# A streaming encoder step: the second half's attention leaves the slots of the first half's output products and norm

## The reference

```python
def sb_attend(q, k, v, q_pos, k_pos):
    z = jnp.einsum('bqhd,bkhd->bhqk', q, k) * (HEAD_DIM ** -0.5)
    mask = k_pos[None, :] < q_pos[:, None]
    log_stay = jnp.where(mask, jax.nn.log_sigmoid(-z), 0.0)
    log_after = lax.cumsum(log_stay, axis=3, reverse=True) - log_stay
    w = jnp.where(mask, jnp.exp(jax.nn.log_sigmoid(z) + log_after), 0.0)
    return jnp.einsum('bhqk,bkhd->bqhd', w, v)
...
        xp = xp + mp          # mp = concat(attention, gating) @ w_out
        xp = xp + swiglu(rmsnorm(xp, norm_ffn[layer]), ffn_w_gate[layer], ffn_w_up[layer], ffn_w_down[layer])
```

## Time and profile before

| | us |
|---|---|
| median of 3 runs | 2579.78 |
| lowest and highest | 2576.31, 2580.04 |
| the profiled execution | 2577.62 |
| its span, first to last instruction | 2575.9 |

### The profile page before, as it was taken

How to read it: one execution, slowest core, us unless ns; L and a number is a source line. 1 busy time by engine, 2 the same in 40 slices (tenths; PEclk the granted TensorE clock), 3 DMA queues, 4 the chain that set the end, 5 groups by cost and what they waited for, 6 DMA issues and landing times.

```text
span 2575.9 us, 39450 instructions
## 1 busy us (share of the span) xinstructions
PE 2488.0 (97%) x15914; PEld 2245.7 (87%) x15914; DVE 1165.3 (45%) x2082; ACT 928.4 (36%) x1336; POOL 1309.6 (51%) x840
## 2 busy tenths in 40 slices
PE   7999889899999999999999999999999999999998
PEld 6999866677878978999999988788888989999998
DVE  6899478655642142444444414535434133223223
ACT  5323367656642332222222424222324243211213
POOL 5466545545446554544434557444445465444444
PEclk9999999899999999999999999999999999999999
DMA  6229772244325454434444232555553223222222
GB/s 192 79 88 329 249 188 67 84 134 116 95 64 196 150 171 125 149 115 124 139 132 140 83 98 75 160 160 151 150 164 95 84 75 107 83 82 82 83 83 70
DMA packets 413732, 322.46 MB, mean 125 GB/s; under 512 B 86560, under 2 KB 370144, under 8 KB 412400
## 3 DMA queue, kind: packets, MB, share of 16 engines
q1 hardware_dynamic: 406464, 292.07, 38.6%
q0 software_dynamic: 5936, 26.69, 2.6%
q10 hardware_dynamic: 1152, 1.18, 0.1%
HBM read 258.78 MB, written 61.10 MB: 124 GB/s over the span
## 4 chain that ended last, share of the span: by engine, by line
PE 88%; DVE 4%; POOL 3%; DMA 2%; issue 1%; ACT 1%; SPq 0%; POOLq 0%; DVEq 0%; ACTq 0%
PE ps L260 26%; PE ps L262 25%; PE ps L261 25%; PE ps L763 3%; PE ps L775 2%; PE ps L1660 1%; PE ps L1654 1%; PE ps L755 1%; POOL wlo L254 1%; PE ps L751 1%; PE ps L1635 1%; DVE nf L1349 1%; DMA mst<-mT 1%; DVE fbuf L346 1%; DMA xA<-xs 0%
## 5 line engine op out<-in xcount | busy, mean ns | idle before, releaser
L254 POOL TENSOR_TENSOR wlo<-raw,whi 128x1024 fp32r<-128x1024 f32 x332 | 800.9, 2416 | 693.6 <-ACT whi L250 692.1
L260 PE MATMUL ps<-hB,whi 128*128 128x320 f32 (+1 forms) x1792 | 535.1, 299 | 4.2 <-POOL lB L1826 3.6
L261 PE MATMUL ps<-lB,whi 128*128 128x320 f32 (+1 forms) x1792 | 531.9, 297 | 0.0
L262 PE MATMUL ps<-hB,wlo 128*128 128x320 f32 (+1 forms) x1792 | 531.8, 297 | 0.0
L250 ACT ACTIVATE whi<-raw 128x1024 fp32r<-128x1024 f32 x332 | 346.6, 1052 | 492.2 <-PE ps L262 377.0
L1312 DVE TENSOR_TENSOR fb<-ps,ab 128x512 f32<-128x512 f32 (+2 forms) x156 | 83.6, 536 | 828.8 <-PE ps L262 738.5
L260 PE MATMUL ps<-hA,whi 128*128 128x512 f32 x896 | 358.3, 400 | 7.7 <-POOL lA L1272 3.9
L260 PE MATMUL ps<-rh,whi 128*128 128x320 f32 (+2 forms) x1032 | 344.5, 334 | 21.3 <-DVE xA L1323 12.2
L261 PE MATMUL ps<-lA,whi 128*128 128x512 f32 x896 | 351.7, 392 | 0.0
L262 PE MATMUL ps<-hA,wlo 128*128 128x512 f32 x896 | 351.1, 392 | 0.0
L260 PEld LDWEIGHTS ps<-hB,whi 128*128 128x128 f32 x1792 | 341.6, 191 | 7.0 <-POOL lB L1826 4.0
(11 more groups left out here) (326 smaller groups left out, 3850.2 us busy)
## 6 DMA issues: line engine op xcount, KB each, us to landing
raw<-in_ffn_w_gate SPq DMA_DIRECT2D x88, 512.0 KB, 3.9
raw<-in_ffn_w_up SPq DMA_DIRECT2D x88, 512.0 KB, 3.9
raw<-in_ffn_w_down SPq DMA_DIRECT2D x88, 512.0 KB, 3.3
raw<-in_ssm_w_glu SPq DMA_DIRECT2D x32, 512.0 KB, 4.1
raw<-in_ab_w_in SPq DMA_DIRECT2D x20, 512.0 KB, 4.5
raw<-in_ab_w_out SPq DMA_DIRECT2D x16, 512.0 KB, 4.2
bt<-dBT SPq DMA_DIRECT2D x16, 512.0 KB, 5.1
tm<-dT SPq DMA_DIRECT2D x16, 512.0 KB, 4.2
```

The lines of the kernel that those rows point to most:

```text
L254: pool.tensor_tensor(wlo[:, slot(t), :], raw[:, t % 2, :], whi[:, slot(t), :].bitcast(F32), ALU.subtract).then_inc(sem("w_lo"), 1)
L260: pe.matmul(out, wh, rh, start=first, stop=False)
L261: pe.matmul(out, wh, rl, start=False, stop=False)
L262: return pe.matmul(out, wl, rh, start=False, stop=last)
```

## The change

The eight outA slots and the two slots of norm tiles take no attention steps. Nothing is added or removed; steps 17 to 28 move behind them, and so every later step moves too.

```diff
             for m in (2 * j, 2 * j + 1):
                 gs = [group("outA", 0, 0, m, [ta])]
-                new_slot(gs, at=some_steps(), sq=squares(gs, 1, 0))
+                new_slot(gs, sq=squares(gs, 1, 0))
         rms_slot(1, 0)
         norm_soon(1, 0, 1, 4)
-        new_slot(at=some_steps())
-        new_slot(at=some_steps())
+        new_slot()
+        new_slot()
```

## The result

The changed kernel takes 2584.93 us (median of 18 runs, 2579.75 to 2590.47). The kernel before, run beside it, takes 2579.11 (18 runs, 2573.57 to 2581.05). The ratio is 1.0022 with a 95% interval of [1.0015, 1.0028]. That is 5.7 us slower, a small effect whose interval lies wholly above 1; the forecast was 9.5 faster. The profiled execution took 2585.33, its span is 2583.6.

What follows compares the result with a forecast made beforehand. PE, busy 97% of the span, was taken to bound the kernel. Gains of 1.8, 6.1 and 1.6 made -9.5 us: 2568.1 profiled, 2570.3 as median of runs, range 2565 to 2575.5, chance 0.60.

Steps and rivals of the forecast that it cites:

- part 2: Second half's norm, slots 89 and 90: PE's waits and the low clock behind them go, 6.1 us gained.
- attention steps and table loads in their new slots: Feed-forward and gate slots: moved steps cost only bare PE time, three more pairs of table loads cost 0.
- Part 1: outA and first norm: without steps there, the norm comes earlier; gain 1.8 us, ends 0.5 and 3.1.
- The middle between the two clock levels: Gate 0's second half: end between 453.6 and 456.2 depending on clock level, taken as 454.9.
- Part 3: Down product at slot 74: the late second weight slab's wait goes, gain 1.6 us, lower end 0.
- The 1.7 for the clock: Behind the second norm's waits: about 3.4 us at low clock, half lost, 1.7 us to be regained.
- Part 4: Stores of pre before hp, later loads and table loads get tighter: cost 0, upper bound 3 us.
- Rival (a): Second norm's stall only moves, colliding elsewhere between slots 94 and 101, or clock loss stays: -3.4, 2576.4 us; chance 0.18.
- Rival (c): Uncovered first norm keeps PE at 1.2 GHz through slots 33 and 34: +8.4 in all, 2588.2 us; chance 0.06.

Runs made afterwards that it cites:

- ap2_s40: Changed kernel with the second half's norm tiles two to a slot and slot 40 without attention steps: 2575.59 us, ratio to before 0.9986.
- noN: Kernel before, with only the two slots of norm tiles (30 and 31) emptied of attention steps: 2585.98 us, ratio 1.0021.
- ap2_s32: Changed kernel with the second half's norm tiles two to a slot and slot 32 (gate 0) without attention steps: 2577.16 us, ratio to before 0.9995.
- late_mix: Kernel before, with only the second half's mixer output, outB, norm and layer 1 preparation ten slots later: 2579.37 against 2578.28 us, ratio 1.0003.

## Why the prediction was wrong, point by point

Two steps failed: part 2, which compared the norm tiles with DVE's deadline alone, and the cost of nothing for attention steps and table loads in their new slots.

**Part 1, outA and first norm: right.** Forecast -1.8. In the ledger, from the last lA to DVE's eviction of up 0, before loses 20.2 (idle 11.3, clock 8.9) and the changed kernel 18.5 (13.6 and 4.9): -1.7. Each time on the way was met within 0.6 us. nf kept the slow pace (up to 1744 ns), as taken. The rule of the Trainium skill weighed there ("SBUF — State Buffer", section "Who interferes with whom": the two kinds of instruction exclude each other) was borne out once more in the second norm, where DVE's pair of nf grew to 3.76 against POOL's slab; the second tile of the pair took 2.68 of it and ended 0.35 behind the slab's conversion:

```profile
986.23 3.76 DVE L1349 SCALAR_TENSOR_TENSOR nf<-xB,cols,mrm 128x320 f32<-128x320 f32 x2 [1.04 <-POOL lB L1299]
```

The middle between the two clock levels for the second half of gate 0 was a guess, and it came out by luck: starts are 0.43 apart until 459.6 and 0.23 behind it. The gain of 1.8 itself is shown by the profiles alone; no run's time isolates it.

**Part 2, second norm: the main step that failed.** Forecast -6.1; measured +4.4 in the ledger's B (9.7 against 5.3). The sentence was "the four tiles that follow up 19, the four beside gate 20 and the kt copies take about 12.3 [...], against the 13.8 until up 20 must be evicted. So the stall goes". The arithmetic for DVE came out (a down group is 6 matmuls, 1.36 us, as part 2 reckons; the 12 in the description of the slots is wrong for down): PE has no wait for an eviction there. But it asked one engine only. The same tiles also stand on ACT and POOL ahead of slot 100's slab, and the down product in slot 101 wants that slab at its first group. Part 3 says in so many words that down is the tight case for slabs; part 2 did not apply it to the down slot that follows its own norm. Two deadlines hung on the same twelve microseconds, and I checked the looser. The 1.7 for the clock was also no property of the kernel: of two profiles of before, one has it and the other has none of it behind the same waits.

**Part 3, slab wait at slot 74: right.** Forecast -1.6; the wait is in none of the profiles whose mixer output comes ten slots later.

**Part 4: right for the stores, in the changed kernel.** hp came in time, the wait of 2.90 at slot 114 is unchanged. One slot more would have cost 4.6 (ap2_s40).

**Put at 0 in the sum: the attention steps in their new slots.** This is the second step that failed. Forecast 0, by "PE has no wait over 0.8 us: these slots are as long as their matmuls. So a step moved there costs its bare PE time", and in part 4 by the table loads in gate slots 66, 70 and 72, "1.28 each, in slots where it has about 8.4 of 9.1 us: 0". A share of busy time doesn't tell whether the load stands just ahead of an exp that PE has nothing to do without: the load behind gate 14 (slot 72) did, and PE waited 1.43. Steps 63 to 66 had moved from down slots to a gate and an up slot. With the 0.55 behind another gate slot and 0.4 more at the last step it is +3.6, between up 0 and slot 74 and without the slab wait (idle 3.5 and clock 1.4 against 1.3 and 0).

Together: -1.7 - 1.6 + 3.6 + 4.4 = +4.7. Between the last lA and the root for hp the profiles show 4.7 (654.5 against 649.8, means of two each). The 60 us behind it give back 1.2, and the runs show 5.7 in all, with an interval of 3.9 to 7.2, so that some 2 us of the loss have no place in this account. Rival (a) was nearest, "if evictions and tiles collide elsewhere between slots 94 and 101", but its price was the old stall at most; a stall that moves can grow. Rival (c) did not occur in the changed kernel, and did, in small, in noN. Its argument against, that the clock came back within 5 us of steady work, was too kind: in the kernel before, PE works from 476.6 on and the level is 0.50 until 482.9, 6.3 us.

What stays open: where those 2 us lie, whether the 3.7 us between ledger and runs in the two versions with two tiles per slot (5.2 against 1.5, just over its uncertainty) has a cause, and what separates ap2_s32 from ap2_s40.

## What to carry to other kernels

When side work is moved in a list that every engine walks in order, ask of its new place for each engine on which it runs what is queued behind it and which slot wants that first; the binding one may be a weight conversion two slots on rather than an eviction beside it. A chain's last links have less of their own work to hide behind than the links in its middle, so the slots in which a chain ends want their own look: what the same engines do just ahead of the link that the next engine waits for, and whether a table is switched there. And where a burst of four tiles causes a stall, spreading it (7 us in both orders here) did what moving it could not.

## What the runs showed of the hardware that I had not expected

- PE's granted clock behind a wait is not a function of the wait alone. Behind 3.08 us of idle time at the same instruction it was 0.50 in one execution and 1.00 in another; behind the same wait of 6.8 for slot 101's slab the loss was 2.8, 2.9 and, in late_mix, 1.5. Behind the wait of 14.69 PE worked 8 us without a break at 0.50 before it was 1.00, behind the one of 3.89 some 4 us. A sum can carry such a loss only as a range: here 0 to 1.7 behind the wait of 3.08 and 1.5 to 2.9 behind the one of 6.8.
- The same instructions up to the last first-half lA ended anywhere from 407.2 to 413.3 us in 14 profiles. The granted clock explains a part of this at most: from 300 to 400 it is 0.90 or 0.91 where lA came at 407.2, 407.9 and 408.7, and 0.87 or 0.88 where it came at 413.1 and 413.3, but the lowest, 0.86, stands with 409.5, 409.8 and 411.7. Two single profiles can't be compared end to end to better than that; distances between common points can.
